# Gated linear attention of the prompt: small blocks for the lower levels, and an output by halves

## What is computed

```python
def _gla(q, k, v, log_a, S0):
    def step(S, inp):
        qc, kc, vc, lac = inp
        cb = jnp.cumsum(lac, axis=1)
        decay = jnp.exp(jnp.where(causal, cb[:, :, None] - cb[:, None, :], -jnp.inf))
        a = jnp.einsum('btshk,bshk->bhts', qc[:, :, None] * decay, kc)
        o = jnp.einsum('bthk,bhkv->bthv', qc * jnp.exp(cb), S) + jnp.einsum('bhts,bshv->bthv', a, vc)
        cl = cb[:, -1]
        S_new = jnp.exp(cl)[..., None] * S + jnp.einsum('bshk,bshv->bhkv', kc * jnp.exp(cl[:, None] - cb), vc)
        return S_new, o
...
    o = _head_rmsnorm(o, g_gla) * jax.nn.silu(gg.astype(F32))
```

## Time and profile before

| | us |
|---|---|
| median of 3 runs | 2767.72 (2766.62 to 2769.05) |
| the profiled execution, its own time | 2768.57 |
| its span | 2766.7 |
| the stage of the change, about | 1794 to 1915 of the span |
| one chunk of it | 14.17 |

### The profile page before, as it was taken

The page is one execution under the profiler, slowest core; times in us unless marked ns, Lnnn a source line. Parts: engine busy times, 40 slices in busy tenths (PEclk is TensorE's granted clock), DMA queues, the critical chain, the costliest instruction groups (busy, mean ns, idle before and its releaser), DMA issues.

```text
span 2766.7 us, 44096 instructions
## 1 busy us (share of the span) xinstructions
PE 2704.3 (98%) x17358; PEld 2479.6 (90%) x17358; DVE 1619.5 (59%) x2131; ACT 1051.6 (38%) x1681; POOL 1338.4 (48%) x764
## 2 busy tenths in 40 slices
PE   8999999989999999999999999999999999999998
PEld 8999988788889988999899989998888999889997
DVE  6943237674676677666743410198367666776665
ACT  5552347463533233323333311365252332333233
POOL 4343455343465565565632131287256555555552
PEclk9999999999999999999999999999999999999999
DMA  6477330235565445554342131034384654445541
GB/s 214 158 249 264 138 129 2 81 119 174 155 234 216 163 151 179 208 203 162 144 146 113 46 137 42 16 115 140 135 245 151 224 215 156 162 167 208 215 172 77
DMA packets 212593, 430.65 MB, mean 156 GB/s; under 512 B 27285, under 2 KB 153585, under 8 KB 201972
## 3 DMA queue, kind: packets, MB, share of 16 engines
q1 hardware_dynamic: 203840, 394.92, 40.7%
q0 software_dynamic: 7776, 31.24, 3.0%
q10 hardware_dynamic: 852, 2.75, 0.3%
HBM read 357.89 MB, written 70.94 MB: 155 GB/s over the span
## 4 chain that ended last, share of the span: by engine, by line
PE 64%; DVE 5%; DMA 3%; issue 2%; POOL 2%; ACT 2%; PEld 0%; PEldq 0%; DVEq 0%; ACTq 0%; SPq 0%; POOLq 0%
PE ps L959 24%; PE ps L1037 22%; PE ps L577 7%; PE ps L638 5%; PE ps L1119 4%; DVE units L4189 1%; DMA units_r<-operands 1%; POOL units_r L718 1%; DMA raw<-w_out 1%; PE ps L3073 0%; ACT ps L3630 0%; DVE spare L4194 0%; POOL split L724 0%; DVE lend L4177 0%; DVE spare L784 0%
## 5 line engine op out<-in xcount | busy, mean ns | idle before, releaser
L1332 POOL TENSOR_TENSOR split<-raw,split 128x1024 fp32r<-128x1024 f32 x218 | 562.0, 2589 | 508.5 <-ACT split L1170 482.9
L959 PE MATMUL ps<-units_r,split 128*128 128x288 f32 x5376 | 720.2, 295 | 12.1 <-POOL split L1332 5.4
L959 PEld LDWEIGHTS ps<-units_r,split 128*128 128x128 f32 x5376 | 717.2, 188 | 15.5 <-POOL split L1332 5.8
L1170 ACT ACTIVATE split<-raw 128x1024 fp32r<-128x1024 f32 x218 | 228.4, 1056 | 465.0 <-PE ps L959 176.9
L1447 DVE TENSOR_TENSOR units<-units,ps 128x512 f32<-128x512 f32 x434 | 285.1, 683 | 121.1 <-PE ps L1037 121.1
L577 PE MATMUL ps<-units_r,split 128*128 128x384 f32 x1872 | 330.4, 336 | 2.3 <-POOL split L290 1.5
L577 PEld LDWEIGHTS ps<-units_r,split 128*128 128x128 f32 x1872 | 326.0, 189 | 3.5 <-issue 1.7
L1037 PE MATMUL ps<-split,units_r 128*128 128x512 f32 x1344 | 309.8, 389 | 0.6 <-DVE units L1447 0.6
L1037 PEld LDWEIGHTS ps<-split,units_r 128*128 128x128 f32 x1344 | 252.0, 188 | 53.9 <-DVE units L1447 1.4
L1037 PE MATMUL ps<-split,spare_r 128*128 128x512 f32 x1008 | 235.6, 389 | 0.0
L1037 PEld LDWEIGHTS ps<-split,spare_r 128*128 128x128 f32 x1008 | 188.5, 188 | 38.5
(11 more groups left out here) (535 smaller groups left out, 4052.3 us busy)
## 6 DMA issues: line engine op xcount, KB each, us to landing
units_r<-operands SPq DMA_DIRECT2D x76, 2304.0 KB, 8.8
raw<-w_ff SPq DMA_DIRECT2D x128, 512.0 KB, 4.3
units_r<-operands SPq DMA_DIRECT2D x22, 1152.0 KB, 7.5
raw<-w_in_even SPq DMA_DIRECT2D x14, 1024.0 KB, 9.3
raw<-w_in_odd SPq DMA_DIRECT2D x12, 1024.0 KB, 5.3
operands<-units_r SPq DMA_DIRECT2D x10, 1152.0 KB, 5.6
operands<-units_r SPq DMA_DIRECT2D x22, 512.0 KB, 3.9
operands<-split SPq DMA_DIRECT2D x18, 512.0 KB, 4.0
```

The costliest lines, as they stand in the source:

```text
L959: last = pe.matmul(ps[:, bank + f, 0:HN], right_slot(base, slot, a)[:, COLS * k + P * f:COLS * k + P * (f + 1)], x[:, b, k, HN * g:HN * (g ...
L1170: act.activation(right_slot(base, slot, 0), src, ACT.Copy).then_inc(hi_ready, 1)
L1332: pool.tensor_tensor(right_slot(base, slot, 1), src, right_slot(base, slot, 0), ALU.subtract).then_inc(lo_ready, 1)
```

## The change

Six things, all in the prompt's GLA.

1. Levels 2 to 7 have nonzero scores only within 32x32 blocks on the diagonal of the 128x128 matrix. TensorE now makes these four blocks alone: for each head four 32x32 products (keys of block g, 32 stationary columns, into partitions 32g to 32g+31; 32 moving columns), instead of one of 128x128. Level 0 is one 64x64 product per head, level 1 two of 32x32.
2. VectorE chooses levels 2 to 7 into a new tile `LA_BLOCKS` of 128 x 4 x 32, with masks folded to 32 columns; level 0 is a plain copy of 64 x 4 x 64 elements and level 1 two copies of 32 x 4 x 32, straight into `LA`.
3. ScalarE copies the four diagonal blocks from `LA_BLOCKS` into `LA` (`gla_blocks`, four instructions of 32 x 4 x 32), between its exponentials of levels 1 and 2 of the next chunk; `gla_out` waits for that.
4. Level 7 comes ahead of the update, on TensorE and VectorE.
5. Output, norm, update and state signal and wait by halves (two heads each): the update of heads 0 and 1 starts when these are read out, and so on.
6. In PT, all of levels 3 to 7 come ahead of the last update.

```diff
+        LEVEL_BLOCKS = ((), (0, 2)) + ((0, 1, 2, 3),) * 6
+        LA_BLOCKS = FKST[:, 0:GH * 32].rearrange("p (h t) -> p h t", h=GH)
...
-                out = ring_bank(e)
+                out = ring_bank(e) if l == 0 else block_bank(e)
                 for h in range(GH):
-                    if l == 7:
-                        last = pe.matmul(out[:, h], GKT[:, h, t], GQ[:, h, t], start=True, stop=True)
-                    else:
-                        last = pe.matmul(out[:, h], levels_in(n)[:, l, h], levels_in(n)[:, l, h], start=True, stop=True)
+                    keys, queries = (GKT[:, h, t], GQ[:, h, t]) if l == 7 else (levels_in(n)[:, l, h],) * 2
+                    if l == 0:
+                        last = pe.matmul(out[0:64, h, 64:P], keys[:, 0:64], queries[:, 64:P], start=True, stop=True)
+                    for g in LEVEL_BLOCKS[l]:
+                        rows = slice(32 * g, 32 * g + 32)
+                        columns_ = slice(32 * g + 32 * (l == 1), 32 * g + 32 * (l == 1) + 32)
+                        last = pe.matmul(out[rows, h], keys[:, rows], queries[:, columns_], start=True, stop=True)
...
-                pe.wait_ge(l_sn, 1 + 4 * n)
-                pe.wait_ge(l_free, ring_taken[ring_place["level", n, 7]])
...
+                pe.wait_ge(l_blocks, BLOCKS0 + n + 1)
+                for b in range(2):
+                    pe.wait_ge(l_sn, 1 + 4 * n - (2 if n and b == 0 else 0))
...
-                pe.wait_ge(l_osc, n + 1)
-                for h in range(GH):
-                    last = pe.matmul(half_banks(h), KST[:, h], GVT[:, n, h * GV:(h + 1) * GV], start=True, stop=True)
-                last.then_inc(l_u, 1)
+                for b in range(2):
+                    pe.wait_ge(l_osc, 2 * n + b + 1)
+                    for h in (2 * b, 2 * b + 1):
+                        last = pe.matmul(half_banks(h), KST[:, h], GVT[:, n, h * GV:(h + 1) * GV], start=True, stop=True)
+                    last.then_inc(l_u, 1)
...
+            def gla_blocks(n):
+                act.wait_ge(l_free, ring_taken[ring_place["level", n, 7]])
+                for g in range(4):
+                    rows = slice(32 * g, 32 * g + 32)
+                    last = act.activation(LA[rows, :, rows], LA_BLOCKS[rows], ACT.Copy)
+                last.then_inc(l_blocks, 1)
...
-                dve.copy_predicated(LA, LEVEL_MASK[:, l].unsqueeze(1).broadcast_to([P, GH, P]), ring_bank(e)).then_inc(l_free, 1)
+                if l == 0:
+                    dve.tensor_copy(LA[0:64, :, 64:P], ring_bank(e)[0:64, :, 64:P]).then_inc(l_free, 1)
+                    return
...
+                dve.copy_predicated(LA_BLOCKS, LEVEL_MASK[:, l, 0:32].unsqueeze(1).broadcast_to([P, GH, 32]),
+                                    block_bank(e)).then_inc(l_free, 1)
```

More of the change, by code:

```diff
@@ L69, in constants @@
     gmask[:, 7] = np.eye(P)
+    for i in range(2, 8):
+        gmask[:, i, 0:32] = np.concatenate([gmask[g:g + 32, i, g:g + 32] for g in range(0, P, 32)])
+        gmask[:, i, 32:] = 0
     later = np.zeros((P, 3, 384), np.float32)
@@ L3125, in _ @@
             for n in range(PT):
-                for l in range(7):
+                for l in range(8):
                     gla_level(n, l)
@@ L3134, in _ @@
                 gla_out(n)
-            for l in range(3, 6):
+            for l in range(3, 8):
                 gla_level(PT, l)
             gla_update(PT - 1)
-            for l in range(6, 8):
-                gla_level(PT, l)
             gla_turn(PT - 1)
@@ L3626, in gla_exp @@
                     x = diff_of(n, l)
+                    if n >= 1 and l == levels_of(n)[2]:
+                        gla_blocks(n - 1)
                     act.wait_ge(l_d, x + 1)
@@ L3675, in gla_norm @@
                                           scale=osum[:, 4 + h:5 + h])
-                last.then_inc(l_osc, 1)
+                    if h % 2:
+                        last.then_inc(l_osc, 1)
             def gla_keys(n):
@@ L4188, in gla_choose @@
                 dve.wait_ge(l_free, ring_taken[e] - 1)
-                dve.copy_predicated(LA, LEVEL_MASK[:, l].unsqueeze(1).broadcast_to([P, GH, P]), ring_bank(e)).then_inc(l_free, 1)
+                if l == 0:
+                    dve.tensor_copy(LA[0:64, :, 64:P], ring_bank(e)[0:64, :, 64:P]).then_inc(l_free, 1)
+                    return
+                if l == 1:
+                    for g in LEVEL_BLOCKS[1]:
+                        rows, columns_ = slice(32 * g, 32 * g + 32), slice(32 * g + 32, 32 * g + 64)
+                        last = dve.tensor_copy(LA[rows, :, columns_], block_bank(e)[rows])
+                    last.then_inc(l_free, 1)
+                    return
+                if n >= 1 and l == max(2, levels_of(n)[0]):
+                    dve.wait_ge(l_blocks, BLOCKS0 + n)
+                dve.copy_predicated(LA_BLOCKS, LEVEL_MASK[:, l, 0:32].unsqueeze(1).broadcast_to([P, GH, 32]),
+                                    block_bank(e)).then_inc(l_free, 1)
             def gla_state(n):
-                dve.wait_ge(l_u, n + 1)
                 for h in range(GH):
+                    if h % 2 == 0:
+                        dve.wait_ge(l_u, 2 * n + h // 2 + 1)
                     dve.scalar_tensor_tensor(out=SS[:, h], in0=SS[:, h], scalar=ecl[:, n % 2, h, 0:1], in1=half_banks(h),
@@ L4202, in gla_mix @@
                     dve.tensor_tensor(v, v, ring_bank(e), ALU.mult).then_inc(l_free, 1)
+            dve.memset(LA_BLOCKS, 0.0)
             after(dve.memset(LA, 0.0))
             for n in range(PT):
-                for l in range(7):
+                for l in range(8):
                     gla_choose(n, l)
```

35 lines of the change are left out of this document (18 added, 17 removed).

## The result

The changed kernel takes **2777.61 us** (2772.66 to 2780.58 in 9 runs) beside 2767.72 for the kernel before (2765.17 to 2771.38 in 9 runs). The ratio is 1.0035, with a 95% interval from 1.0027 to 1.0044: slower, by 0.35%. The forecast was 2753, and the range ended at 2766. Both were wrong, and so was the sign.

A forecast was written before the change was run, and what follows sets the result against it. TensorE (13.88) and VectorE (13.36) fill a 14.17 us pass, GpSimd's 11.79 being the next bound. Seven passes save 15.4, the end 1.1, a clock fall costs 1.7: 14.8 off, 2753 against 2767.72; range 2748 to 2766.

The forecast's parts named there:

- The loop: Chunk pass through VectorE, TensorE and ScalarE, from choose 0 to the next: 14.16 us before, 11.96 after, saving 2.2.
- The block products: TensorE's 32x32 products in levels 2 to 7: a round of four below 0.07 us, a level well under 0.5.
- The rounds do not shrink: Rival, chance 0.18: a TensorE round stays at 0.11 us with 32 moving columns; 0.7 saved a pass, about 2765.
- the products do not run side by side: Rival, chance 0.05: TensorE's block products run serially, 1.7 us a level, 18.5 a chunk; about 2802.
- VectorE's chooses: Chooses of levels 2 to 7 at 128 elements: 0.42 us each, 3.6 for all eight levels against 6.6.
- ScalarE's copies: Four block copies per chunk ahead of the output: between 0.8 and 1.2 us together, ended by F+6.6 (F: choose 0 begins).
- TensorE's levels: Step pricing each level's 32 small records by array time: 0.22 to 0.87 us a level, plus about 0.5 for width changes.
- The clock falls in the stage: Rival, chance 0.06: lower TensorE work and half-microsecond holes bring 1.2 GHz; all stage long +4 a chunk, about 2799.
- one fall of 1.7: Chunk 0's output: TensorE idles 4 us before the block copies, so one clock fall costs 1.7 us.
- Chunks 0 and 1: Stage start: chunk 0 gains nothing and a clock fall costs 1.7 us; chunk 1's pass saves 2.2.
- The end: Last update to `keep_clock`: update starts 0.75 us sooner, then 4.85 where 5.19 stood; gain 1.1.
- a wait I don't see: Catch-all rival, chance 0.05: an unseen wait, place not named, eats most of the gain.

The follow-up runs named there:

- e1: The changed kernel with 44 tiny 32x32 products (176 instructions) added once ahead of chunk 0: 2759.46 us, ratio 0.9966 to the kernel before.
- e3: The changed kernel with 64x64 blocks for levels 1 to 7, 324 TensorE instructions a chunk instead of 516: 2750.43 us, ratio 0.9936 to the kernel before.
- e2: The changed kernel with 64 tiny 32x32 products (256 instructions) added once ahead of chunk 0, as control of e1: 2780.68 us, ratio 1.0045.
- e7: e3 with 48 tiny products (192 instructions) ahead of each chunk's update, 516 instructions a chunk again: 2769.14 us, ratio 1.0003 to the kernel before.
- e4: The changed kernel with full 128x128 products, 512-element chooses and no block copies, keeping the new order and halves: 2766.93 us, ratio 0.9997.
- e5: e3 with the halves undone: output, norm, update and state wait for all four heads: 2761.09 us, ratio 0.9974 to the kernel before.

## Why the prediction was wrong

**The loop was right.** The forecast was 11.96 a pass. Where TensorE does not pause, e1 (the very chunks of the change) shows 12.06, with GpSimd at 11.74 of it. Its first update record starts at F+2.96, ended by ScalarE, and the next factors at F+6.95, where 2.85 and 6.85 were put.

**The block products were right.** A level was to take well under 0.5. Level 7's 32 records take 0.46 in e1 (also at the end of the stage in after). In the timeline above, the 64 records of levels 5 and 6 begin at 1845.92 and level 7 at 1846.65: 0.73 for two levels of eight rounds each, so 0.046 a round where a value below 0.07 was put, and 0.011 from one record's start to the next. *The rounds do not shrink* and *the products do not run side by side* both fall: the first wanted 0.87 a level (0.80 by the rule that it names), the second 1.7; it was 0.37.

**VectorE's chooses and ScalarE's copies were right.** The five chooses of 128 elements behind levels 2 to 6 and the block copies, VectorE and ScalarE of after:

```profile
1845.87 1.94 DVE L4225 COPY_PREDICATED key_rows<-sel,ps 128x128 f32<-128x128 uint32 x5
1848.72 0.30 DVE L4225 COPY_PREDICATED key_rows<-sel,ps 128x128 f32<-128x128 uint32 x1 [0.91 <-PE ps L3087]
...
1850.28 1.25 ACT L3641 ACTIVATE units<-key_rows 32x128 f32<-32x128 f32 x4
```

1.94 for five is 0.39 each where 0.42 was put; a single one is 0.30; the copies take 1.25, just above the upper bound of 1.2. The second row also shows where it went wrong: VectorE sits idle 0.91 for level 7, which by the forecast is done long before.

**The step that failed** is the one headed TensorE's levels. It took the cost of a product to be its time in the array, and set the burst at what the array needs. The number of instructions went from about 212 to 516 a chunk, and 432 of them (216 records and their weight loads) stand in the levels, which the array could end in some 4 us. The fetching of the instructions was not in the sum at all: it was put at nothing without a reason. What the runs showed in its place is a pause in each chunk of 1.32 to 4.71, 20.5 us together, until the next block is there. Levels 3 to 7 were allowed 3.0 before they delay the update; from level 3's start to the update they take 3.85 to 5.27 in the six passes of after. The order's rows gave the count, and the earlier trace rows the speed: four records and seven weight loads start within 0.06 us, which I read as proof of a cheap level and not as a rate at which blocks of 256 are used up. Before, 256 instructions lasted over a chunk, 17 us, so a block that comes within 8 us is never late.

**The clock.** *The clock falls in the stage* came true in part, though not by its own reason. I priced it by TensorE's lower share of work and by holes of half a microsecond. Those holes are in e3's passes too, with TensorE busy 11.25 of 12.07 and the clock at 1.00. In e1 TensorE is busy 10.32 of 12.06 and waits 0.9 in one place, at 1.00. In the middle of the stage the falls of after stand beside pauses of 1.49 to 2.62, which were not foreseen, so a chance of 0.06 stood for something else. As a bound the 2.32 of the earlier trace rows fails both ways: the fall at 1863.2 follows an idle 2.02, while e2 kept 1.00 behind 2.02 and 2.18 and e7 behind 3.48. And for chunk 0 I charged one fall of 1.7. The windows there show more, first of before, then of after:

```profile
1794.90:1798.30 3.40, 3.40 (x33) 3.40 (x32) 2.86 (x4) 1.54 (x4) 2.39 (x2) 1.00 0.85 293
1801.70:1805.10 3.40, 2.99 (x14) 2.69 (x15) 3.05 (x10) 1.80 (x3) 3.40 (x7) 1.00 1.02 403
```

```profile
1794.90:1798.30 3.40, 1.72 (x115) 1.56 (x101) 1.93 (x7) 1.18 (x3) 2.76 (x3) 0.50 0.93 312
1798.30:1801.70 3.40, 0.55 (x29) 0.51 (x29) 0.00 (x0) 1.20 (x2) 3.40 (x7) 0.50 1.05 400
1801.70:1805.10 3.40, 2.55 (x12) 1.89 (x8) 2.62 (x9) 2.50 (x7) 3.40 (x7) 0.50 1.03 407
1805.10:1808.50 3.40, 3.40 (x9) 2.70 (x8) 2.58 (x8) 2.98 (x8) 3.40 (x7) 0.50 1.02 392
```

Four such stretches, 13.6 us, at 1.2 GHz, where before had none. The first began at 1794.90, ahead of the pause that starts at 1796.6, so the pause did not cause that one. Nor did the small products by themselves: e4, which has the products of before, has 0.50 from 1795.9 to 1799.3.

**The sum, again.** Forecast 14.8 less, measured 11.9 more: 26.7 missed.
- Six passes: forecast 13.2 less, measured 90.0 - 85.4 = 4.6 more. That is 17.8 of it. Against e1's 12.06 the six exceed by 17.6. The pass of 13.05 has a pause of 1.32 and a full clock, and exceeds by 1.0, so 0.33 of a pause is covered. The six pauses are 2.02, 1.32, 2.02, 1.49, 2.62 and 1.81, 11.3 together, less 0.33 each: 9.3. The other 8.3 go with the clock. This split is worked out. For the pauses' part speak the two passes of e2 at clock 1.00: pauses of 2.02 and 2.18 made them 1.65 and 1.84 longer, so 0.37 and 0.34 were covered there.
- Chunks 0 and 1: forecast 0.5 less (1.7 more, 2.2 less), measured 6.5 more (1823.65 against 1817.19). That is 7.0, with the two longest pauses and the slow stretches of above:

```profile
1801.15 0.64 PE L3087 MATMUL ps<-units 128*32 128x32 f32 x29 [4.53 <-issue]
...
1817.48 0.44 PE L3087 MATMUL ps<-units 128*32 128x32 f32 x14 [4.71 <-issue]
1817.85 3.78 PE L3108 MATMUL ps<-units,glrow 128*128 128x256 f32 x8
```

- The end: forecast 1.1 less, measured 0.6 less (11.49 against 12.10 from the last factors to `keep_clock`). The last update starts 0.62 sooner behind the factors (6.29 for 6.91), where 0.75 was put, and from there to `keep_clock`, which waits for the block copies, idle 1.92, it is 5.20, where 4.85 was put. That is 0.5.
- Behind the stage: 1.4, not traced.

The chance of 0.05 for "a wait I don't see" was what came, and it ate more than the gain. The profile of before gives only a part of its price: its seven packets in the stage (0.4% of 16 engines in 121 us) take 1.1 us each, but TensorE never used up a block fast enough there to wait, so the delays before and behind the packet don't show. But the two counts were at hand, and an unpriced resource whose use rises by 2.4 is a rival with a place of its own, not a remainder.

The Trainium skill does name it. "Runtime: NRT & Kernel Launch", in Instruction fetch mechanics, says that instructions come in blocks of 16 KiB, 256 of them, that the next is fetched while the current one runs, and that crossing an edge is mostly hidden. The packets of 16 KB and the 512 instructions from pause to pause agree with the size, and the packets' starts in the table with a fetch that runs beside the current block. "Mostly hidden" does not hold in this burst: 1.3 to 4.7 us were open at every second edge.

**What stays open.** What sets the 0.85 to 1.90 us until the packet starts where nothing else moves. That other transfers lengthen it to 2.39 to 5.27 is read from four pauses; no run changed the transfers alone. Which pauses bring a lower clock. And why the clock fell at 1794.90; e1 and e3 fall there too.

## What to carry to other kernels

Count an engine's instructions beside its busy time: here each fp32 product costs four, and bursts in which 256 instructions last some 2 us stood still for 1.3 to 4.7 us at their end, while 324 a chunk, with products of 64x64 and twice the elements, took 17 us off the kernel of before. The trace has the price: the next block came 3.4 to 4.1 us after the start of the one before it, and 4.7 to 8.0 beside other transfers. A wait ended by "issue" that returns after a fixed number of instructions is the sign, and a one-time shift of the stream by part of a block (e1, 21 us away from e2) is the cheap test for it. A part that frees nothing alone (the halves, e4) can be worth 1.5 a pass once another part has opened the bound (e3 beside e5).

## What the runs showed of the hardware

- Small products in four groups of 32 rows: 64 records and their 64 weight loads start within 0.73, about 6 ns an instruction.
- Instructions came in packets of 16 KB, one for 256. The packet of the next block started 0.85 to 1.90 us after the start of the current block at a DMA share of at most 0.06, 2.39 to 5.27 at 0.87 or more, and TensorE went on 2.2 to 2.8 us after the packet's start (nine pauses, after and e7).
- The time of this kernel depends on how many instructions TensorE has run before the stage: 176 more gave 2759.46, 256 more gave 2780.68.
- The clock kept 1.00 in a pass with TensorE busy 10.32 of 12.06 and a hole of 0.87 at its start. In after, the pause of 1.32 was followed by an update at full speed (1.99), that of 2.02 in chunk 4 by one that took 3.02 with a stretch at 0.50. In e2 a pause of 2.18 and in e7 one of 3.48 were followed by 1.00.
